# One core, a three-block transformer in split fp32: late gain rows at the beginning, dt on GpSimd, the last z later, and retention's values multiplied among the heads

## The reference

```python
def swiglu(h, w_gate, w_up, w_down):
    return (jax.nn.silu(h @ w_gate) * (h @ w_up)) @ w_down

# block 1: x += 0.5 swiglu(rms_norm(x)); x += mamba2(rms_norm(x)); x += 0.5 swiglu(rms_norm(x))
#   mamba2: proj = h @ w_in;  z, xbc, dt = proj
#           xbc = silu(conv4(xbc));  dt = softplus(dt + dt_bias);  y = ssd(xs, dt, a, B, C) + d_skip * xs
#           g = y * silu(z);  g = g * rsqrt(mean over 256 (g*g) + eps) * norm_w;  out = g @ w_out
# block 2: the same with multi-head latent attention in the middle
# block 3 (second_block):
(mq, mk, mv, mo, mi, mf, dq, dk, dv, rq, rk, rv, rg, gates) = split_in(rmsnorm(x) @ w_in)
hm = sigmoid(mo) * head_rms(mlstm(...))
hd = rmsnorm(diff_attention(dq, dk, dv, lam), diff_subln) * (1 - lam_init)   # 8 heads, a = p1 - lam * p2
hr = silu(rg) * head_rms(retention(rq, rk, rv))                              # 4 heads
gm, gd, gr = split(sigmoid(gates))
y = (gm * (hm @ w_mlstm_out) + gd * (hd @ w_diff_out) + gr * (hr @ w_ret_out)) @ w_out
x = x + rmsnorm(y);  x = x + rmsnorm(swiglu(rmsnorm(x)))
```

## Time and profile before

| what | before |
|---|---|
| median of three runs | 1828.56 us |
| profiled execution, its span | 1827.93 us, 1826.2 us |
| PE busy | 1751.2 us (96%) |
| DVE, ACT, POOL busy | 1233.4, 868.4, 70.8 us |
| mean granted clock of PE | 0.982 |
| DMA | 298.26 MB, mean 163 GB/s |

### The profile page before, as it was taken

How to read it: one execution, slowest core, us unless ns; L and a number is a source line. 1 busy time by engine, 2 the same in 40 slices (tenths; PEclk the granted TensorE clock), 3 DMA queues, 4 the chain that set the end, 5 groups by cost and what they waited for, 6 DMA issues and landing times.

```text
span 1826.2 us, 24702 instructions
## 1 busy us (share of the span) xinstructions
PE 1751.2 (96%) x9513; PEld 1505.2 (82%) x9513; DVE 1233.4 (68%) x1418; ACT 868.4 (48%) x1056; POOL 70.8 (4%) x122
## 2 busy tenths in 40 slices
PE   7999999989999999998899999999998899989998
PEld 6888889878888888887678888987886687878887
DVE  5666798665766677667657676875657474567676
ACT  5444565755444444446444444755345434445443
POOL 0000001120000000002000000001000000000000
PEclk9999999989999999999799999999999899999999
DMA  6655455324655565544216654554552265436552
GB/s 223 198 185 197 141 176 169 108 88 139 207 186 195 170 200 191 184 152 167 69 47 209 198 191 154 185 184 138 185 185 70 92 208 161 162 115 230 196 184 92
DMA packets 213089, 298.26 MB, mean 163 GB/s; under 512 B 12374, under 2 KB 168603, under 8 KB 213019
## 3 DMA queue, kind: packets, MB, share of 16 engines
q1 hardware_dynamic: 213018, 297.30, 49.8%
HBM read 296.21 MB, written 1.05 MB: 163 GB/s over the span
## 4 chain that ended last, share of the span: by engine, by line
PE 87%; DVE 6%; ACT 4%; issue 2%; DMA 1%; POOL 1%; SPq 0%; DVEq 0%; POOLq 0%; ACTq 0%
PE PS L437 26%; PE PS L443 13%; PE PS L338 11%; PE PS L339 11%; PE PS L393 7%; PE PS L357 4%; PE PS L428 2%; PE PS L429 2%; PE PS L430 2%; PE PS L332 1%; PE PS L334 1%; PE PS L333 1%; ACT whi L316 1%; DVE wlo L321 1%; PE PS L679 1%
## 5 line engine op out<-in xcount | busy, mean ns | idle before, releaser
L321 DVE TENSOR_TENSOR wlo<-raw,whi 128x2048 fp32r<-128x2048 f32 (+1 forms) x284 | 640.7, 2259 | 168.5 <-ACT whi L316 167.9
L316 ACT ACTIVATE whi<-raw 128x2048 fp32r<-128x2048 f32 (+1 forms) x284 | 536.3, 1890 | 438.4 <-PE PS L443 307.8
L437 PE MATMUL PS<-XT,whi 128*128 128x512 f32 x2016 | 506.8, 394 | 5.4 <-DVE XT L741 3.7
L437 PEld LDWEIGHTS PS<-XT,whi 128*128 128x128 f32 x2016 | 368.2, 190 | 75.1 <-issue 4.2
L443 PEld LDWEIGHTS PS<-XT,wlo 128*128 128x128 f32 x2016 | 274.2, 191 | 18.9
L443 PE MATMUL PS<-XT,wlo 128*128 128x256 f32 x2016 | 280.9, 283 | 0.0
L339 PE MATMUL PS<-whi,aT 128*128 128x512 f32 x400 | 156.3, 391 | 0.0
L338 PE MATMUL PS<-whi,aT 128*128 128x512 f32 x400 | 156.2, 390 | 0.0
L338 PE MATMUL PS<-whi,XT 128*128 128x512 f32 (+2 forms) x320 | 126.1, 395 | 1.2 <-ACT V L1914 1.1
L339 PE MATMUL PS<-whi,XT 128*128 128x512 f32 (+2 forms) x320 | 123.1, 386 | 0.0
L578 ACT ACTIVATE aT<-ff_a 128x512 fp32r<-128x512 f32 x50 | 31.6, 631 | 170.9 <-PE PS L393 162.5
(11 more groups left out here) (410 smaller groups left out, 2262.6 us busy)
## 6 DMA issues: line engine op xcount, KB each, us to landing
raw<-in_w_in SPq DMA_DIRECT2D x112, 512.0 KB, 4.5
raw<-in_ffn_w_gate SPq DMA_DIRECT2D x88, 512.0 KB, 4.5
raw<-in_ffn_w_up SPq DMA_DIRECT2D x88, 512.0 KB, 4.4
raw<-in_ffn_w_down SPq DMA_DIRECT2D x88, 512.0 KB, 4.1
raw<-in_ssm_w_in SPq DMA_DIRECT2D x48, 512.0 KB, 4.6
raw<-in_w_ffn_in SPq DMA_DIRECT2D x44, 512.0 KB, 4.2
raw<-in_w_ffn_out SPq DMA_DIRECT2D x22, 512.0 KB, 4.1
raw<-in_ssm_w_out SPq DMA_DIRECT2D x16, 512.0 KB, 4.4
```

The lines of the kernel that those rows point to most:

```text
L316: act.activation(whi[s][:, 0:size], raw[s][:, 0:size], ACT.Copy).then_inc(hi_done, 1)
L321: dve.tensor_tensor(wlo[s][:, 0:size], raw[s][:, 0:size], whi[s][:, 0:size].bitcast(FP32), ALU.subtract).then_inc(lo_done, 1)
L437: return pe.matmul(o, whi[n % SLOTS][:, sl], XT[:, k, :, :].rearrange("p a n -> p (a n)"), start=(k == 0), stop=False)
```

## The change

Five parts. (a) Beginning: x is loaded in column halves, block 0 in three parts, norm_w's rows by ACT's queue; the other rows follow block 1, are turned by PE after the gate of the first layer (at L527 of the new file) and copied by ACT after rstd's row; a new mul_start_pairs takes the place of mul_first_pairs in the first layer. (b) dt_quotient and dt_value move from DVE to POOL, where the reciprocal becomes a power of -0.5, squared; DVE waits for dt at i = 4 and does the sums at i = 4, 6 and 8; PE turns at i = 8. (c) The last z is evicted after group 6's exponentials in place of after group 5. (d) In the heads of differential attention DVE's order is new, 1/sum of the first softmax is taken out of AW and multiplied into the final scale, and ACT splits ahead of the exponentials. (e) Retention's values are loaded between the halves of gd and multiplied in the heads (32 steps in place of 16) into a tile of their own, RV; ACT evicts gd and rv in the heads; the stretch for retention's values after its features is gone.

```diff
-        N["gd"] = natural_blocks(in2, C_G + DM, 2)
+        N["gd"] = natural_blocks(in2, C_G + DM, 1)
+        N["rv"] = natural_blocks(in2, C_RV, 1)
+        natural_blocks(in2, C_G + DM + 512, 1)
+        natural_blocks(in2, C_RV + 512, 1)
...
+        def mul_start_pairs(pe, gate, up):
+            first, second = range(KD // 2), range(KD // 2, KD)
+            pe.wait_ge(half_hi, 1)
+            for k in first:
+                pe.wait_ge(*normed(0, k))
+                for c in range(2):
+                    high_by_both(pe, gate[:, c, :], 0, c, k)
+            turn_x(pe, 0, 1)
+            pe.wait_ge(half_lo, 1)
...
+            spread_rstd(pe, 0, PS[:, 0, 0:SEQ])
+            pe.wait_ge(s_rows, 16 * (len(NROW) - 1))
+            for i in range(3):
+                pe.transpose(ROWS_AT[i], rows[i][0:ROWS_IN[i], :], ident[0:ROWS_IN[i], 0:ROWS_IN[i]]).then_inc(s_rowt, 1)
+            wait_high(pe, 1)
...
+        def start_act(act, at):
...
+            high(range(KD // 2))
+            act.wait_ge(half_in, 16)
+            act.activation(whi[0][:, 0:half], raw[0][:, 0:half], ACT.Copy).then_inc(half_hi, 1)
+            act.wait_ge(x_in[0], 16 * NT)
+            act.wait_ge(x_in[1], 16 * NT)
+            for t in range(NT):
+                act.activation(xn[:, t, :], xs_[:, t, :], ACT.Square, accum_out=stat[:, t:t + 1]).then_inc(S["sq_done"], 1)
+            act.wait_ge(raw_loaded[0], 32)
+            act.activation(whi[0][:, half:BLK], raw[0][:, half:BLK], ACT.Copy).then_inc(hi_done, 1)
+            high(range(KD // 2, KD))
...
-                if i == 6:
+                if i == 8:
                     pe.wait_ge(A["dta"], 1)
...
+                if g == 6:
+                    evict_z(3)
                 hi_upto(act, at, nz + Z_AHEAD[g + 1])
...
-                if g in (-1, 2, 5):
+                if g in (-1, 2):
+                    evict_z((g + 4) // 3)
...
-                if i == 1:
-                    dt_quotient()
-                if i == 2:
-                    dt_value()
-                if i == 3:
+                if i == 4:
                     decay_sums()
+                if i == 6:
+                    sums_hi()
+                if i == 8:
+                    sums_lo()
...
+            def dt_quotient():
+                pool.wait_ge(A["e"], 2)
+                own.link(pool.tensor_scalar(hrow[:, H_D, :], hrow[:, H_E, :], 1.0, -1.0, ALU.add, ALU.add))
+                own.link(pool.tensor_scalar(hrow[:, H_Q, :], hrow[:, H_D, :], 1e-30, None, ALU.max))
+                own.link(pool.tensor_tensor(hrow[:, H_Q, :], hrow[:, H_Q, :],
+                                            neghalf[0:SSM_HEADS, 0:1].to_broadcast([SSM_HEADS, SEQ]), ALU.pow))
+                own.link(pool.tensor_tensor(hrow[:, H_Q, :], hrow[:, H_Q, :], hrow[:, H_Q, :], ALU.mult))
+                own.link(pool.tensor_tensor(hrow[:, H_Q, :], hrow[:, H_E, :], hrow[:, H_Q, :], ALU.mult))
...
+        FILL = [0, 4, 8, 11, 14, 17, 20, 23, 26, 29, 32]
+        def filled(h):
+            return N["gd"] + min(FILL[h] // 4 + 2, 8)
+        def fill_steps(pe, h):
+            free = (B["cp"], 3), (B["cp"], 4), (B["gev"], 5), (B["cp"], 5)
...
             for h in range(DH + 1):
+                hi_upto(act, at, filled(h))
...
+                if h in (2, 8):
+                    c = h // 8
+                    act.wait_ge(block_used, N["gd"] + 4 * c + 2)
...
+                    act.activation(GT[:, :, c * 512:(c + 1) * 512], PS[:, 0:2, :], ACT.Sigmoid).then_inc(B["gev"], 1)
+                if h == 5:
+                    retention_values(act, 0)
...
-                        m = dve.tensor_scalar(AW[:, sl], U[:, u, 0, sl], dsum[:, u, t, 0:1], None, ALU.mult)
-                    own.link(m)
+                        m = dve.scalar_tensor_tensor(out=AW[:, sl], in0=U[:, u, 1, sl], scalar=dmix[:, t:t + 1],
+                                                     in1=U[:, u, 0, sl], op0=ALU.mult, op1=ALU.add)
...
+            x_half(0)
+            first_block(0, 4, half_in)
+            x_half(1)
+            first_block(4, 2, raw_loaded[0])
+            first_block(6, 2, raw_loaded[0])
+            stream(1, 2)
+            for src, r, at in NROW[1:]:
```

More of the change, by code:

```diff
@@ L495, in mul_first_pairs @@
             m.then_inc(block_used, 1)
+        def mul_start_pairs(pe, gate, up):
[7 more added lines that the diff above has]
+            pe.wait_ge(half_lo, 1)
+            for c in range(2):
+                for k in first:
+                    low_by_high(pe, gate[:, c, :], 0, c, k)
+            wait_high(pe, 0)
+            for k in second:
+                pe.wait_ge(*normed(0, k))
+                for c in range(2):
+                    high_by_both(pe, gate[:, c, :], 0, c, k)
+            wait_block(pe, 0)
+            for c in range(2):
+                for k in second:
+                    m = low_by_high(pe, gate[:, c, :], 0, c, k)
+            m.then_inc(block_used, 1)
+            spread_rstd(pe, 0, PS[:, 0, 0:SEQ])
[3 more added lines that the diff above has]
+            wait_high(pe, 1)
+            for c in range(2):
+                for k in range(KD):
+                    high_by_both(pe, up[:, c, :], 1, c, k)
+            wait_block(pe, 1)
+            for c in range(2):
+                for k in range(KD):
+                    m = low_by_high(pe, up[:, c, :], 1, c, k)
+            m.then_inc(block_used, 1)
+            pe.wait_ge(s_rowc, 4)
         def mul_first_features(pe, n, norm, banks=PS[:, 2:4, :]):
@@ L544, in flat @@
             return a[:, :, :].rearrange("p c n -> p (c n)")
+        ROWS_AT = [PS[:, 7, i * P:i * P + ROWS_IN[i]] for i in range(3)]
         GATE, UP = PS[:, 6:8, :], PS[:, 4:6, :]
@@ L581, in ffn_act @@
             row_act(act, norm, PS[:, 0, 0:SEQ])
+            if norm == 0:
+                act.wait_ge(s_rowt, 4)
+                for r in range(3):
+                    act.activation(cols[r][:, COLS_AT[r]:ROWS_IN[r]], ROWS_AT[r][:, COLS_AT[r]:], ACT.Copy)\
+                       .then_inc(s_rowc, 1)
             silu(0)
@@ L674, in turn_x @@
             else:
-                for t in range(NT):
-                    pe.wait_ge(x_in[t], 16)
+                pe.wait_ge(x_in[c], 16 * NT)
             for k in range(c * KD // 2, (c + 1) * KD // 2):
@@ L1775, in values_T @@
             return pe.matmul(PS[:, 7, 0:width], W[:, 2 * P:TRI], v[:, 1, :], start=False, stop=True)
+        FILL = [0, 4, 8, 11, 14, 17, 20, 23, 26, 29, 32]
[3 more added lines that the diff above has]
+            free = (B["cp"], 3), (B["cp"], 4), (B["gev"], 5), (B["cp"], 5)
+            step = FILL[h]
+            while step < FILL[h + 1]:
+                b, s0 = step // 4, step % 4
+                s1 = min(4, s0 + FILL[h + 1] - step)
+                pair = b // 2 % 2
+                if b % 2 == 0 and s0 == 0:
+                    pe.wait_ge(*free[b // 2])
+                mul_rows(pe, N["gd"] + b, 0, 4 * (b % 2), 4, 512, [psD[:, 2 * pair + t, :] for t in range(NT)],
+                         b % 2 == 0, b % 2 == 1, part=range(s0, s1))
+                step += s1 - s0
         def b2_pe(pe):
@@ L1929, in squares_act, with diff_squares @@
                 act.activation(ff_s[:, t, 0:width], banks[t], ACT.Square, accum_out=oss[:, i, t:t + 1]).then_inc(B["sq"], 1)
+        def diff_squares(act, g):
+            i = LH + g
+            act.wait_ge(B["o"], i + 1)
+            for t in range(NT):
+                act.activation(ff_s[:, t, 0:P], psS[:, t * P:(t + 1) * P], ACT.Square, scale=dinv[:, g % 4, t:t + 1],
+                               accum_out=oss[:, i, t:t + 1]).then_inc(B["sq"], 1)
         def pair_banks(i):
@@ L2006, in b2_act @@
                 if h >= 2:
-                    squares_act(act, LH + h - 2, P, [psS[:, 0:P], psS[:, P:2 * P]])
-            squares_act(act, LH + DH - 1, P, [psS[:, 0:P], psS[:, P:2 * P]])
-            for c in range(2):
-                gate_act(act, at, N["gd"], c, ACT.Sigmoid, (B["yv"], 1))
+                    diff_squares(act, h - 2)
+            diff_squares(act, DH - 1)
+            retention_values(act, 1)
             left_act(act, B, HTh, 4)
@@ L2212, in b2_dve @@
                         dve.wait_ge(B["aw"], h - 1)
-                    own.mark(dve.scalar_tensor_tensor(out=U[:, h % 2, :, :],
+                    own.link(dve.scalar_tensor_tensor(out=U[:, h % 2, :, :],
                                                       in0=dist[:, :].unsqueeze(1).to_broadcast([P, 2, TRI]),
@@ L2416, in _ @@
             at, own = Position(), Chain(act, act_own)
-            hi_upto(act, at, 0)
-            for i in range(3):
-                act.wait_ge(s_rowt, i + 1)
-                act.activation(cols[i][:, 0:ROWS_IN[i]], PS[:, 2 + i, 0:ROWS_IN[i]], ACT.Copy).then_inc(s_rowc, 1)
-            act.wait_ge(s_rowc, 3)
-            norm_act(act, 0, 0)
+            act.dma_start(rows[0][0:48, :], NROW[0][0]).then_inc(s_gain, 16)
+            act.wait_ge(s_rowt, 1)
```

(3 more changed lines are left out.)

196 lines of the change are left out of this document (104 added, 92 removed).

## The result

The changed kernel takes 1822.07 us (median of nine runs, 1820.30 to 1823.01), the kernel before beside it 1832.24 us (nine runs, 1826.24 to 1834.41). The ratio is 0.9955, 95% interval 0.9942 to 0.9968: 0.45% faster, where the forecast was 1791.5 us, outside the predicted range of 1784 to 1818. The profiled execution has a span of 1818.9 us, 7.3 less than before.

A forecast was written before the change was run, and what follows sets the result against it. PE, busy 96% of the span, was taken as the bound, so gains lie only at its waits or half-clock time. Gains of 6.5 + 4.0 + 3.5 + 23 = 37 us gave 1791.5 us, range 1784 to 1818.

The forecast's parts named there:

- The step that failed: dt on GpSimd: the 32x256 power costs about a same-width multiplication, 0.63 us, not 39.8 us by its slope.
- Rival (1): Conv loop: the power follows its slope, dt comes at 277.6, 25 us worse than forecast, 1816.5 us; chance 0.27.
- Its dt at 277.6: Conv loop, first rival: dt ready at 230.8 + 2 + 39.8 + 5 = 277.6 us, no split disturbing POOL.
- The beginning: Kernel start: halved loads let weight products start at 8.4 us, second gate group near 23; gain 6.5 us.
- The last z: Last ssm groups: evicting z after the exponentials removes PE's 2.92 us wait; gain 3.5 us, bounds 1 and 5.
- the two microseconds for products at half clock: Last ssm groups: 16 products after PE's second wait, now at half clock, were worth another 2 us.
- The heads: Differential attention heads and retention's values: a net gain of 23 us, 26 with 6.5 a head, 20 with 7.5.
- The stretch of 23.0 us: Retention's values: their own stretch, 4 blocks and the wait for V, goes; 23.0 us.
- The head at 7.0 us: Differential attention: a middle head takes 7.0 us, between 6.5 at least and 7.5 if DVE's round is never hidden.
- The reason given for 6.5: Differential attention: PE's own 2.4 us a head plus 3 filling steps of 1.36 us make 6.5 us.
- the sum of four terms: Whole kernel: beginning 6.5, dt 4.0, last z 3.5, heads and retention 23, together a gain of 37 us.
- the power's term: Conv loop: dt on GpSimd arrives in time and removes PE's waits for low parts; gain 4.0 us.

The follow-up runs named there:

- the last z alone: Kernel before with part (c) alone, the last z evicted after the last exponentials: 1829.88 us, ratio 1.0004.
- the order alone: Kernel before with only DVE's new order in the heads, two filling steps a head and retention's values in their old stretch: 1825.96 us, ratio 0.9975.
- dt on DVE: Changed kernel with part (b) undone, dt's quotient and value on DVE again: 1797.62 us, ratio 0.9817 to the kernel before.

## Why the prediction was wrong

**The step that failed** is the one on the power: "I take the row that is nearest in size: a step of 154 ns over one to four columns can be the latency of a short loop, which 256 columns can fill." There is no such filling. The instruction's own rows gave a slope of 154 ns a column; the chip has 159 to 161, over a range of 256 columns. The forecast had worked out 39.8 us from it, measured were 41.15, and it then preferred a multiplication's row because its shape was the same. The term was +4.0 and came as -23.4, 27.4 us of the 30.6 between 1791.5 and 1822.07.

**Rival (1) was the truth**, with a chance of 0.27, and its steps hold: the low part of a block is late, and the term is -21 with it, measured -23.4. Its dt at 277.6 is in the time of before; the measured 276.5 lies 6.0 us behind the earlier beginning, so it is 282.5 in that time. Of the 4.9 us between the forecast's time and this the power began 2.1 later (POOL's second instruction took 2.89 us beside a split), took 1.35 more, and the eight instructions behind it 6.4 in place of 5.

**The beginning** was forecast as 6.5 and is 6.0 in the trace, and with this part alone 6.3 by the first group's power. Its steps hold: first weight product 8.4 (8.86), second group of gate products near 23 (24.55; 22.95 to 24.09 in the five experiments with this beginning). The rows of gains were turned without a wait at 18.68, so the second block covered them.

**The last z** was forecast as 3.5 and is 1.8 with the rest of the change and 1.0 alone, where the whole kernel is no faster. The wrong part is the two microseconds for products at half clock: with the wait of 2.92 us gone the clock fell all the same, and in the last z alone 12 products of the projection run at 1.2 GHz in place of 4.

**The heads** were forecast as 23 and are 27.0. The stretch of 23.0 us is gone as worked out. The head at 7.0 us was mis-sized: it is 6.46, which the forecast had as the least. That is 6 x 0.54 = 3.2 of the 4.0 missing. The forecast had the heads 3.9 us longer than before; from the first scores to the first turn of xn they take 72.6 us in place of 73.1. The reason given for 6.5 was PE's own work; the order alone shows 6.46 with only two steps of that work and a wait of 1.4 for xn, so the round between PE and DVE (values, turn and scores on PE, U to xn on DVE) has the same length, and a third step, 1.36 us, just fills the wait. And the two halves were not weighed apart: the filling makes the gain, with the order of before it is 26.8.

**Ahead of all** stood the sum of four terms. With the power's term replaced (the multiplication in its place, 1790.8 us; the reciprocal on DVE, 1791.6 us) the sum of 37 us is right (span 1788.9 against 1826.2, 37.3), though by errors that cancel. With the multiplication, 6.5 come at the beginning as forecast and 6.2 from dt, 2.2 more than forecast. The last z gives 1.8, 1.7 less, and the heads 27.1, 4.1 more; 3.3 are lost in the latent attention, where the change has no instruction, and 1.0 in the rest. Without the unsure border behind the beginning, dt comes out a little smaller: the first group's power is 12.7 us earlier than before with the multiplication and 7.3 with dt on DVE, so part (b) is worth 5.4.

On 32x256 a multiplication took 603 ns and the power 41152, 68 times as long. The rule that the prediction quoted from the Trainium skill (GPSIMD Engine Reference, section Elementwise — side-by-side cycle accounting, about 2.6 cycles per element) is right for the first and says nothing of the second. The small instructions of dt on POOL take 0.6 to 1.1 us, and 2.66 to 2.90 beside a split of DVE; the power takes 41.15 with three splits or with eight in it. The same page, section Key points, says that GpSimd contends with VectorE when that reads two inputs in SBUF, as a split does: the small instructions agree, and so do the powers that began in a split (up to 2.04 us longer), but splits that began during a power did not lengthen it.

## What to carry to other kernels

When an instruction's cost must be guessed, the rows of the same operation at another size outrank the row of another operation at the same size: extrapolate the slope first. A slow instruction on an idle engine is free until somebody waits for it, so look at what is queued behind the waiting instruction, and put the wait where its data will be; here that alone was worth 28 us. And when a change has a filler and a new order in it, test each alone: the filler gave 26.8 of 27.0 us.
